# Two TensorE read streams of a hybrid decoder trunk: columns taken from the last to the first, hi and lo parts interleaved, weight slots staggered by 32 bytes

## What is computed

```python
h = h + stick_breaking_mixer(rmsnorm(h, sb_norm), sb_w_qkv, sb_w_o)     # 2048 x 6144, 2048 x 2048
h = h + swiglu_ffn(rmsnorm(h, ffn_norm[0]), w_gate_up[0], w_down[0])    # 2048 x 11264, 5632 x 2048
h = h + chunked_gmlp_mixer(rmsnorm(h, gm_norm), gm_w_in, ..., gm_w_o)   # 2048 x 4096, 2048 x 2048
h = h + swiglu_ffn(rmsnorm(h, ffn_norm[1]), w_gate_up[1], w_down[1])
return rmsnorm(h, final_norm)

def swiglu_ffn(h, w_gate_up, w_down):
    gate, up = jnp.split(h @ w_gate_up, 2, axis=-1)
    return (jax.nn.silu(gate) * up) @ w_down
```

## Time and profile before

| | |
|---|---|
| Time, median of 2 runs | 2097.78 us (2097.65 to 2097.91) |
| Profiled execution: span, first to last instruction | 2097.8 us |
| Of it PE busy | 2088.2 us, in 9281 records |
| PE's weight loads (PEld) busy | 1729.4 us |
| DVE, ACT busy | 1430.7 us, 1013.1 us |
| From HBM | 399.55 MB read, 191 GB/s over the span |
| Mean granted TensorE clock | 0.999 of full speed |

### The profile page before, as it was taken

The page is one execution under the profiler, slowest core; times in us unless marked ns, Lnnn a source line. Parts: engine busy times, 40 slices in busy tenths (PEclk is TensorE's granted clock), DMA queues, the critical chain, the costliest instruction groups (busy, mean ns, idle before and its releaser), DMA issues.

```text
span 2097.8 us, 27159 instructions
## 1 busy us (share of the span) xinstructions
PE 2088.2 (100%) x9281; PEld 1729.4 (82%) x9281; DVE 1430.7 (68%) x1822; ACT 1013.1 (48%) x1285; POOL 16.4 (1%) x30
## 2 busy tenths in 40 slices
PE   9999999999999999999999999999999999999998
PEld 7888888888888888888888888888888888888887
DVE  6787777867666676665557887877666676664444
ACT  6577765544444444444445444554444444444443
POOL 1000000000000000000000000000000000000000
PEclk9999999999999999999999999999999999999999
DMA  8555554666666666555566665566666666655554
GB/s 264 179 179 170 181 189 167 198 196 192 191 190 198 191 193 195 192 191 196 194 192 209 190 200 183 190 190 201 192 189 198 192 193 194 190 194 198 192 191 150
DMA packets 207419, 402.47 MB, mean 192 GB/s; under 512 B 12336, under 2 KB 13056, under 8 KB 206976
## 3 DMA queue, kind: packets, MB, share of 16 engines
q1 hardware_dynamic: 206496, 398.11, 61.1%
q0 software_dynamic: 688, 3.18, 0.4%
q10 hardware_dynamic: 176, 0.40, 0.1%
HBM read 399.55 MB, written 2.10 MB: 191 GB/s over the span
## 4 chain that ended last, share of the span: by engine, by line
PE 99%; issue 0%; DMA 0%; DVE 0%; ACT 0%; POOLq 0%; POOL 0%; DVEq 0%; SPq 0%
PE acc L1085 64%; PE acc L1091 32%; PE tp L1156 0%; PE tp L1176 0%; PE acc L1106 0%; PE acc L1107 0%; PE acc L1108 0%; PE tp L1302 0%; DMA h<-in_x 0%; PE tp L1116 0%; PE acc L1345 0%; PE acc L1344 0%; PE acc L1343 0%; PE acc L1143 0%; PE tp L1136 0%
## 5 line engine op out<-in xcount | busy, mean ns | idle before, releaser
L654 DVE TENSOR_TENSOR w_lo<-raw,w_hi 128x1024 fp32r<-128x1024 f32 x750 | 916.0, 1224 | 584.9 <-ACT w_hi L348 581.1
L348 ACT ACTIVATE w_hi<-raw 128x1024 fp32r<-128x1024 f32 x750 | 792.9, 1060 | 922.4 <-PE acc L1091 917.2
L1085 PE MATMUL acc<-w_hi,xT 128*128 128x512 f32 x4032 | 998.7, 390 | 0.0
L1085 PEld LDWEIGHTS acc<-w_hi,xT 128*128 128x128 f32 x4032 | 756.0, 188 | 155.9
L1091 PE MATMUL acc<-w_lo,xT 128*128 128x512 f32 x2016 | 539.2, 389 | 0.0
L1091 PEld LDWEIGHTS acc<-w_lo,xT 128*128 128x128 f32 x2016 | 378.6, 188 | 78.5
L1085 PE MATMUL acc<-w_hi,hid_hi 128*128 128x512 f32 x944 | 368.7, 391 | 0.0
L1085 PE MATMUL acc<-w_hi,hid_lo 128*128 128x512 f32 x944 | 367.6, 389 | 0.0
L1091 PE MATMUL acc<-w_lo,hid_hi 128*128 128x512 f32 x944 | 252.5, 389 | 0.0
L1091 PEld LDWEIGHTS acc<-w_lo,hid_hi 128*128 128x128 f32 x944 | 177.3, 188 | 36.7
L1085 PEld LDWEIGHTS acc<-w_hi,hid_hi 128*128 128x128 f32 x944 | 177.3, 188 | 36.8
(11 more groups left out here) (115 smaller groups left out, 477.6 us busy)
## 6 DMA issues: line engine op xcount, KB each, us to landing
raw<-in_ffn_w_gate_up SPq DMA_DIRECT2D x352, 512.0 KB, 4.5
raw<-in_ffn_w_down SPq DMA_DIRECT2D x176, 512.0 KB, 3.6
raw<-in_sb_w_qkv SPq DMA_DIRECT2D x95, 512.0 KB, 4.3
raw<-in_gm_w_in SPq DMA_DIRECT2D x64, 512.0 KB, 4.4
raw<-in_sb_w_o SPq DMA_DIRECT2D x32, 512.0 KB, 4.1
raw<-in_gm_w_o SPq DMA_DIRECT2D x32, 512.0 KB, 4.0
h<-in_x SPq DMA_DIRECT2D x3, 512.0 KB, 7.6
gain_bc<-in_gm_v_norm POOLq DMA_DIRECT2D x1, 1024.0 KB, 6.1
```

The costliest lines, as they stand in the source:

```text
L348: nc.scalar.activation(w_hi[:, p % RING], raw[:, p % RING], ACT.Copy).then_inc(hi_ready, 1)
L654: nc.vector.tensor_tensor(w_lo[:, p % RING], raw[:, p % RING], w_hi[:, p % RING].bitcast(f32), ALU.subtract).then_inc(lo_ready, 1)
L1085: nc.tensor.matmul(acc_at(chunk, r), part[:, kt, rs], w_hi[:, p % RING, k], start=(kt == 0 and part is hi), stop=False)
```

## The change

It does five things.

- **Columns reversed.** Every one of the 9024 matmuls reads its 512 weight columns from the last to the first (`back`) and writes its sums into PSUM from the last to the first (`acc_back`), so that each sum stands where it stood. The stationary operand isn't reversed.
- **Parts alternating.** `xT` and the inner activations (now one tensor, `hid`) hold high and low part of a token side by side: a stationary operand is 128 elements with a step of 8 bytes, over 1024 bytes, where it was 128 elements in a row, over 512. ACT and DVE write them with that step. The total size is the same; the tensors that share `region` move accordingly (`FREE`, `MORE`).
- **Slots staggered.** Each slot of `w_hi` and `w_lo` is followed by 64 unused bytes, and there are 32 between the two tensors. Measured from the activations, modulo 256 bytes, the slots of `w_hi` begin at 0, 64, 128 and 192 and those of `w_lo` at 32, 96, 160 and 224. The slots of `raw` stay.
- **`region`** still lies at a multiple of 512 bytes from `w_hi`.
- **PE's loops are written out**, all but that of the up projections (line 1257 before).

```diff
-        xT = sb("xT", [P, KD, 2, S], f32r)
-        xT_hi, xT_lo = xT[:, :, 0], xT[:, :, 1]
+        xT = sb("xT", [P, KD, S, 2], f32r)
+        xT_hi, xT_lo = xT[:, :, :, 0], xT[:, :, :, 1]
         raw = sb("raw", [P, RING, KP, CH])
-        w_hi = sb("w_hi", [P, RING, KP, CH], f32r)
-        w_lo = sb("w_lo", [P, RING, KP, CH], f32r)
+        STAGGER = 16
+        w_hi = sb("w_hi", [P, RING, KP * CH + STAGGER], f32r)[:, :, 0:KP * CH].rearrange("p s (k n) -> p s k n", k=KP)
+        w_gap = sb("w_gap", [P, STAGGER // 2])
+        w_lo = sb("w_lo", [P, RING, KP * CH + STAGGER], f32r)[:, :, 0:KP * CH].rearrange("p s (k n) -> p s k n", k=KP)
...
-        hid_hi = at("hid_hi", 0, [P, KF, S], f32r)
-        hid_lo = at("hid_lo", HB, [P, KF, S], f32r)
+        hid = at("hid", 0, [P, KF, S, 2], f32r)
+        hid_hi, hid_lo = hid[:, :, :, 0], hid[:, :, :, 1]
...
-        FREE = KD * S * 4
+        FREE = 2 * KD * S * 4
+        MORE = FREE + (KF - KD) * S * 4
...
+        def acc_back(chunk, rt):
+
+            return acc[:, ::-1][:, bass.ds((2 * RT - 1 - rt) * CH - half(chunk) * (RT * CH), CH)]
+
+        def back(t, slot, k):
+
+            return t[:, slot, k, ::-1]
...
-                                nc.tensor.matmul(acc_at(chunk, r), part[:, kt, rs], w_hi[:, p % RING, k],
+                                nc.tensor.matmul(acc_back(chunk, r), part[:, kt, rs], back(w_hi, p % RING, k),
                                                  start=(kt == 0 and part is hi), stop=False)
...
-                            last = nc.tensor.matmul(acc_at(chunk, r), hi[:, kt, r * P:(r + 1) * P],
-                                                    w_lo[:, p % RING, k], start=False, stop=(kt == K - 1))
+                            last = nc.tensor.matmul(acc_back(chunk, r), hi[:, kt, r * P:(r + 1) * P],
+                                                    back(w_lo, p % RING, k), start=False, stop=(kt == K - 1))
...
-            with pe.Fori(1, ND) as j:
+            for j in range(1, ND):
                 qkv_round(j)
```

More of the change, by code:

```diff
@@ L103, in hybrid_trunk @@
         moments = sb("moments", [P, RT, 2])
+        W0 = nc.lookup_mloc(raw).addr + RING * KP * CH * 4
         used_up_to = nc.lookup_mloc(moments).addr + 32
-        lead_in = sb("lead_in", [P, (nc.lookup_mloc(w_hi).addr - used_up_to) % CH // 4])
+        lead_in = sb("lead_in", [P, (W0 - used_up_to) % CH // 4])
         region = sb("region", [P, 2 * KF * S])
         R0 = nc.lookup_mloc(region).addr
-        assert (R0 - nc.lookup_mloc(w_hi).addr) % CH == 0
-        HB = KF * S * 4
+        assert (R0 - W0) % CH == 0
         def at(name, offset, shape, dt=f32):
             return nc.alloc_sbuf_tensor_at(name, shape, dt, offset=R0 + offset)
-        hid_hi = at("hid_hi", 0, [P, KF, S], f32r)
-        hid_lo = at("hid_lo", HB, [P, KF, S], f32r)
+        hid = at("hid", 0, [P, KF, S, 2], f32r)
+        hid_hi, hid_lo = hid[:, :, :, 0], hid[:, :, :, 1]
         rows_first = at("rows_first", 0, [KD, P])
-        FREE = KD * S * 4
+        FREE = 2 * KD * S * 4
+        MORE = FREE + (KF - KD) * S * 4
         CB = RT * CH * 4
@@ L131, in hybrid_trunk @@
         probT = at("probT", FREE + 5 * CB + 3 * ZB, [P, ZW])
-        prob_blk = at("prob_blk", HB + FREE + 5 * CB, [P, ZW])
+        prob_blk = at("prob_blk", MORE + 5 * CB, [P, ZW])
         left = at("left", FREE + 5 * CB + 4 * ZB, [P, ZW + 2])
[L134 to L137, removed]
+        q_t = at("q_t", MORE, [P, HG, S])
+        k_t = at("k_t", MORE + CB, [P, HG, S])
+        vn = at("vn", MORE, [P, RT, D])
+        wsT = at("wsT", MORE + RT * D * 4, [P, KD, P])
         ws_raw = at("ws_raw", FREE, [P, KD, P])
@@ L1104, in piece @@
                         rs = slice(r * P, (r + 1) * P)
[L1105 to L1108, removed]
+                        dst = acc_back(chunk, r)
+                        nc.tensor.matmul(dst, hi[:, kt, rs], back(w_hi, p % RING, k), start=(kt == 0), stop=False)
+                        nc.tensor.matmul(dst, hi[:, kt, rs], back(w_lo, p % RING, k), start=False, stop=False)
+                        last = nc.tensor.matmul(dst, lo[:, kt, rs], back(w_hi, p % RING, k), start=False,
                                                 stop=(kt == K - 1))
@@ L1240, in residual_rest @@
             def residual_rest(which, base, hi, lo, first):
-                with pe.Fori(first, ND) as c:
+                for c in range(first, ND):
                     for p in range(PD):
@@ L1286, in _ @@
                 piece(AT_GMI, 0, 2 * PD, t, c, p * KP, KD, xT_hi, xT_lo)
-            with pe.Fori(2, ND) as c:
+            for c in range(2, ND):
                 pe.wait_ge(gelu_ready, c - 1)
@@ L1306, in _ @@
             u_chunk(0, True)
-            with pe.Fori(1, ND) as c:
+            for c in range(1, ND):
                 u_chunk(c, False)
@@ L1336, in _ @@
                 rs = slice(r * P, (r + 1) * P)
-                dst = acc_at(1, r)
+                dst = acc_back(1, r)
                 for t in range(ROWWISE, 2 * PF):
@@ L1342, in _ @@
                         kt = (t - PF) * KP + k
-                        nc.tensor.matmul(dst, hid_hi[:, kt, rs], w_hi[:, t % RING, k], start=False, stop=False)
-                        nc.tensor.matmul(dst, hid_hi[:, kt, rs], w_lo[:, t % RING, k], start=False, stop=False)
-                        last = nc.tensor.matmul(dst, hid_lo[:, kt, rs], w_hi[:, t % RING, k], start=False,
+                        nc.tensor.matmul(dst, hid_hi[:, kt, rs], back(w_hi, t % RING, k), start=False, stop=False)
+                        nc.tensor.matmul(dst, hid_hi[:, kt, rs], back(w_lo, t % RING, k), start=False, stop=False)
+                        last = nc.tensor.matmul(dst, hid_lo[:, kt, rs], back(w_hi, t % RING, k), start=False,
                                                 stop=(kt == KF - 1))
```

## The result

2162.11 us (2 runs, 2162.09 to 2162.13) against 2097.78 before: 1.0307 times as long, 95% interval 1.0277 to 1.0337. The change makes the kernel slower by 3%. I had forecast 2022 us, faster by 3.6%: the sign is wrong, and the time lies in the band of the third case, the load paying for its bytes (2140 to 2260 us). The stated range, 1998 to 2200 us, holds it, but only because it was drawn over cases of both signs; to slower I had given 0.33.

What follows compares the result with a forecast made beforehand. PE was taken to bound the kernel: 9024 matmuls going from 226.7 to 218.3 ns save 75.8 us, other terms 0, so 2097.8 becomes 2022 us. The range was 1998 to 2200 us.

Steps and rivals of the forecast that it cites:

- the third case: Rival for all 9024 matmuls: loads pay by bytes spanned, 237.4 ns each, 2195 us (band 2140 to 2260); chance 0.31.
- cases of both signs: Forecast outcomes for the whole kernel: faster, under 2056 us, 0.45; same 0.22; slower 0.33.
- The bound: Whole kernel: PE alone bounds it, 9024 matmuls at 226.7 ns making 2046 us of the 2097.8.
- What the 13.3 ns are: Each matmul's excess over 213.3 ns: 10.8 ns of it read as load and stream hindering each other in SBUF, 97 us.
- the equal pace: Load and stream passing SBUF at the same rate, as in the attention's four-pass matmuls, claimed to make a load cost 2.5 ns.
- Reversed and alternating: All 9024 matmuls: both reads at one rate, keeping their distance, 226.7 to 218.3 ns, saving 75.8 us.
- The low and high bounds of that state: Load's cost per matmul: 2.5 ns as in the attention's four-pass rows, or 5 ns for twice the bytes; 5 taken.
- the likeliest case: All 9024 matmuls gain from reads at one rate: 2022 us, range 1998 to 2056; chance 0.45.
- PSUM written backward: Sums of every matmul written from last column to first: claimed to cost nothing.
- the fourth case: Rival on PSUM: backward sums go one column per 1.2 GHz cycle, 1.8 ms more, some 3.9 ms; chance 0.02.
- ACT, DVE and DMA: Activation writes with a step might grow by 1 us a piece, hidden by ACT's 1.66 us idle; DMA 0.
- The two rules: Skill's claims: independent read ports with 215.8 ns per matmul, meaning no gain; two hits per 16-byte line make the step free.

Runs made afterwards that it cites:

- e_pairs: Kernel before with PE's loops written out, stream reading 256 weight columns twice each instead of 512; another product: 2005.18 us.
- e_rev_pairs: Kernel before with PE's loops written out, stream reading 256 weight columns twice each, backward, sums written forward; another product: 2005.56 us.
- e_alt: Kernel before with PE's loops written out and high and low parts alternating, nothing reversed or staggered: 2157.59 us, 233.3 ns a matmul.
- e_revalt: The changed kernel without the stagger, so reversed and alternating with slots as before: 2170.93 us, 234.8 ns a matmul.
- e_cols32: Kernel before with PE's loops written out; all but first and last matmul of a sum load 32 columns, not 128; another product: 2141.16 us.
- e_revw: Kernel before with PE's loops written out and weight columns read backward, sums written forward; another product: 2157.17 us, 233.3 ns.
- e_step4: Kernel before with PE's loops written out, load taking every fourth element (16-byte step, 2048 bytes); another product: 2173.64 us, 235.1 ns.
- e_revacc: Kernel before with PE's loops written out and only sums written backward into PSUM; another product: 2097.94 us, 226.7 ns.
- e_move0: Kernel before with PE's loops written out, stream reading one weight column 512 times; another product: 2021.25 us.
- e_rev: Kernel before with PE's loops written out, weight columns read and sums written backward, no alternating, no stagger: 2156.82 us, 233.2 ns.
- e_rev_load0: Kernel before with PE's loops written out, weights read backward, sums forward, each load reading one column 128 times; another product: 2157.13 us.
- e_rev_cols32: Kernel before with PE's loops written out, mostly 32-column loads, weights read and sums written backward; another product: 2157.07 us, 233.3 ns.
- e_load0: Kernel before with PE's loops written out, each load reading one column 128 times; another product: 2128.01 us, 230.0 ns.
- e_off4: Kernel before with PE's loops written out, weight slots 252, 0, 4 and 8 bytes off a multiple of 256: 2139.98 us.

## Why the prediction was wrong

**The bound.** Right: PE is 99% of the chain before and after, and the whole difference is the distance between its matmuls.

**What the 13.3 ns are.** This is the step that failed. I read the earlier trace rows as "a load costs 2.5 ns when the stream is read at the load's own pace", and took the equal pace for the cause. Another thing that sets those matmuls apart is that their stream takes new bytes from SBUF at half the rate. e_pairs alone can't tell the two apart: with 256 columns in the same time its stream also moves at the load's pace. But no row shows in which direction a load runs, and whichever it is, of e_pairs and e_rev_pairs one has the two reads side by side and the other has them head on; both are at 215.8 ns. At the full rate it is the same the other way round: of e_alt and e_revalt one has the two side by side at equal pace, and they are at 233.3 and 234.8. So half the rate makes those matmuls cheap, and the equal pace doesn't. And the earlier trace rows, from which I took that the two reads hinder each other, shows only that the distance depends on how they stand to each other. e_cols32 shows that this isn't a price per read of the load: with a quarter of it the distance goes up, to 231.5. What the 13.3 ns are physically stays open.

**Reversed and alternating.** I charged 218.3 ns for the two; they stand at 234.8 together and at 233.3 each. The low and high bounds of that state, 2.5 and 5 ns, were built on the wrong cause, so nothing held up the range of the likeliest case (1998 to 2056).

**The third case**, slower by the load's bytes, had the sign and a band that held the time, but not the mechanism. That its band held the time is luck. Its own check, a spacing above 226.7 in all slots alike, came true but for part of slot 0; the price it gave to the change was 237.4 ns, where 233.8 came. e_revw gets to 233.3 with the old load, and e_step4, at four times the bytes, is 235.1 where 10.8 ns for each 512 bytes give 259. What I should have kept apart is the sign of a change of layout and the reason given for it.

**Slots.** I took the stagger for a part that costs nothing by itself. Alone it costs 4.9 ns a matmul, 44 us: the kernel before is at the one good distance found, and the stagger leaves it. With reversed and alternating parts there is nothing left to lose, and it gives 8.8 us back (2170.93 to 2162.11).

**PSUM written backward**: nothing, as I took it (e_revacc, 226.7); the fourth case is out. The rows it drew on, show 512 columns in 0.43 us, the pace of 1.2 GHz, but the profile gives a granted clock of 1.00 for 7 to 10 us too: its rise is not to be seen in it. **Loops**: nothing, as said (e_revacc again, 2097.94 us against 2097.91). **ACT, DVE and DMA**: covered, as said; ACT sits idle 1.75 us a piece in place of 1.66, and its writes with a step took 12% and 4% longer, not twice as long.

**The two rules.** "TensorE: Matmul & The Clock Gate" of the Trainium skill ("Back-to-back issue gap") gives 215.8 ns for 512 columns, for what it calls an isolated matmul, and e_pairs measures just that in a stream, so here the rule holds for a stream with half the new bytes and not for this fp32r stream at its full rate, at 226.7 at best. The two independent read ports of the same page ("Step-by-step: what each phase is for") fit with e_cols32, where a shorter load brings nothing; but the same stream stands at 226.7, 230.0, 231.5, 233.3 or 235.1 by nothing but the shape of the load beside it, so the two are not without effect on each other. "Advanced Engine Details and Errata" of the Trainium skill ("SBUF Cachelines") would have let the 8-byte step of the load and the backward read go free, since both hit each line at least twice. They cost 6.6 ns each, so the traces don't agree with it.

**Still open.** Why a contiguous load at a distance of exactly 0 makes a forward stream cheaper (226.7) than every other arrangement measured at the full rate, in the mean of a piece (229 to 240), and what the stream would cost with no load beside it; every kernel here has one before each matmul. That the load's address and shape move the distance is shown; whether the two contend for SBUF, or something else links them, is not, and why a backward read and a step of 8 bytes each come to the same 233.3 isn't known either. None of the kernels that compute the whole product is faster than the one before.

## What to carry to other kernels

The fp32r stream of this kernel doesn't run at its column rate (226.7 ns at best for 512 columns, where 213.3 would do): in such a kernel look at the distance between starts (12 matmuls in 2.72 us, not the mean duration), and compare it with the same kernel reading half the new bytes. If a tuned kernel sits at a small fraction over that floor, its SBUF places may already be at a narrow optimum, and each change of address, step or direction has to be measured alone before it is combined. A cheap row differs from a dear one in more than one respect: name them all, before one is made the cause.

## What the runs showed of the hardware

- A matmul that streams 512 fp32r columns, with a load beside it, takes 215.8 ns from start to start if each of 256 columns is read twice (e_pairs), 217.5 if it is always the same one (2.61 us for twelve in e_move0), and 226.7 at best if all are new.
- Two distances return to the tenth: 226.7 ns (the kernel before, e_revacc) and 233.3 (e_rev, e_revw, e_alt, e_rev_load0, e_rev_cols32). At the granted 2.4 GHz they are 544 and 560 periods, 32 and 48 more than there are columns. Elsewhere the distance goes round in patterns of two to four values, as 230.9, 226.1, 233.5 in e_load0.
- 4 bytes above the good place cost 10 ns a matmul (e_off4), by estimate 4% of this kernel if all its slots stood there; 4 bytes below cost 2.
- Sums can be written into PSUM from the last column to the first at no cost (e_revacc, 2097.94 us against 2097.91).
